# Copies and adds for the Strassen weight sums on new places, low parts of the first blocks on VectorE, and another order of the tail

## What is computed

```python
def first_block(x, p, ...):
    h = rmsnorm(x, g_pre)
    (qa, ka, va, gate_a, qi, ki, wi, qb, kb, vb, fb, gate_b) = split(h @ w_in)
    att_a = dsa_branch(qa, ka, va, qi, ki, wi)      # sparse attention, 8 heads
    att_b = fox_branch(qb, kb, vb, log_f)           # forgetting attention, 8 heads
    m_a, m_b = split(sigmoid(h @ w_merge))
    out = (m_a * (att_a * silu(gate_a)) @ w_branch_a + m_b * (att_b * silu(gate_b)) @ w_branch_b) @ w_out
    x = x + rmsnorm(out, g_post)
    return x + rmsnorm(sigmoid(x @ w_ple_gate) * (p @ w_ple), g_ple)

def second_block(x, ...):
    h = rmsnorm_2(x, mix_norm_g)
    qa, ka, va, q_lat, kv_lat, k_r, g_a, g_b = split(h @ w_in)
    o_a = swa_sink_attention(qa, ka, va, sinks)     # sliding window, 8 heads
    o_b = mla_attention(q_nope, q_rope, k_nope, k_rope, v)      # 8 heads
    y = sigmoid(g_a) * (o_a @ w_o_swa) + sigmoid(g_b) * (o_b @ w_o_mla)
    x = x + y @ w_out
    h = rmsnorm_2(x, ffn_norm_g)
    x = x + (silu(h @ w_gate) * (h @ w_up)) @ w_down            # d_ff 2816
    return rmsnorm_2(x, final_norm_g)
```

## Time and profile before

| What | Value |
|---|---|
| median of 3 runs | 1210.23 us (1209.99 to 1212.33) |
| the profiled execution | 1208.32 us, span 1206.5 us |
| PE busy | 1166.1 us, 97% of the span |
| DVE, ACT, POOL busy | 819.9 us (68%), 630.9 us (52%), 411.5 us (34%) |
[...]
| DMA: SP's queue, POOL's queue | 180.46 MB and 30.41 MB |

### The profile page before, as it was taken

How to read it: one execution, slowest core, us unless ns; L and a number is a source line. 1 busy time by engine, 2 the same in 40 slices (tenths; PEclk the granted TensorE clock), 3 DMA queues, 4 the chain that set the end, 5 groups by cost and what they waited for, 6 DMA issues and landing times.

```text
span 1206.5 us, 17475 instructions
## 1 busy us (share of the span) xinstructions
PE 1166.1 (97%) x6392; PEld 1000.5 (83%) x6392; DVE 819.9 (68%) x1663; ACT 630.9 (52%) x1105; POOL 411.5 (34%) x287
## 2 busy tenths in 40 slices
PE   9999999999999799999899999899989999999996
PEld 8878778888888687789778788688879999998885
DVE  5789874774628237699981775672599878786575
ACT  6553574476522345448683787333364454544454
POOL 1428462445544334312362676345435000000000
PEclk9999999999999899999999999999999999999998
DMA  8216773713998996555321402787546666667871
GB/s 276 79 63 244 210 244 141 227 53 140 287 274 230 298 280 192 163 207 147 106 39 37 140 1 69 213 208 176 138 156 199 206 204 202 205 218 256 312 261 70
DMA packets 91092, 216.30 MB, mean 179 GB/s; under 512 B 18424, under 2 KB 28152, under 8 KB 83968
## 3 DMA queue, kind: packets, MB, share of 16 engines
q1 hardware_dynamic: 83232, 180.46, 44.6%
q0 software_dynamic: 4608, 30.41, 12.4%
q10 hardware_dynamic: 3168, 4.33, 1.0%
HBM read 198.24 MB, written 71.45 MB: 224 GB/s over the span
## 4 chain that ended last, share of the span: by engine, by line
PE 71%; DVE 15%; DMA 4%; ACT 3%; issue 3%; POOL 2%; SPq 0%; ACTq 0%; DVEq 0%; POOLq 0%
PE bank L2302 38%; PE bank L2624 14%; PE bank L2638 8%; PE bank L2366 3%; PE bank L2398 2%; PE bank L2380 2%; PE bank L2444 2%; DVE sc L1789 2%; DMA w_raw<-in_w_out 1%; DVE m L1785 1%; DVE sqS L1935 1%; DMA w_raw<-in_w_o_mla 1%; POOL w_lo L907 1%; DVE t_lo L2023 1%; DMA rot<-in_rot 1%
## 5 line engine op out<-in xcount | busy, mean ns | idle before, releaser
L888 POOL TENSOR_TENSOR w_lo<-w_raw,w_hi 128x2048 fp32r<-128x2048 f32 (+4 forms) x49 | 218.1, 4451 | 366.3 <-ACT w_hi L992 311.8
L2302 PE MATMUL bank<-aH,w_hi 128*128 128x512 f32 x544 | 218.7, 402 | 2.6 <-DVE mqT L1986 1.0
L2302 PE MATMUL bank<-aH,w_lo 128*128 128x512 f32 x544 | 212.4, 391 | 0.0
L2302 PE MATMUL bank<-aL,w_hi 128*128 128x512 f32 x544 | 205.8, 391 | 0.0
L992 ACT ACTIVATE w_hi<-w_raw 128x2048 fp32r<-128x2048 f32 (+4 forms) x45 | 82.9, 1843 | 128.3 <-PE bank L2302 94.9
L2624 PE MATMUL bank<-t_hi,w_hi 128*128 128x256 f32 x504 | 143.5, 285 | 6.0 <-POOL w_lo L977 3.6
L2624 PE MATMUL bank<-t_hi,w_lo 128*128 128x256 f32 x504 | 143.1, 284 | 0.0
L2624 PE MATMUL bank<-t_lo,w_hi 128*128 128x256 f32 x504 | 143.1, 284 | 0.0
L2302 PEld LDWEIGHTS bank<-aH,w_hi 128*128 128x128 f32 x544 | 102.6, 189 | 22.2 <-issue 4.4
L2302 PEld LDWEIGHTS bank<-aL,w_hi 128*128 128x128 f32 x544 | 102.1, 188 | 22.3
L2302 PEld LDWEIGHTS bank<-aH,w_lo 128*128 128x128 f32 x544 | 102.5, 188 | 16.3
(11 more groups left out here) (414 smaller groups left out, 2687.2 us busy)
## 6 DMA issues: line engine op xcount, KB each, us to landing
w_raw<-in_w_in SPq DMA_DIRECT2D x21, 1024.0 KB, 5.0
w_raw<-up_sums SPq DMA_DIRECT2D x36, 512.0 KB, 4.3
w_raw<-in_gate_up SPq DMA_DIRECT2D x35, 512.0 KB, 4.2
up_sums<-in_gate_up SPq DMA_DIRECT2D x16, 1024.0 KB, 7.8
w_raw<-in_w_merge SPq DMA_DIRECT2D x8, 1024.0 KB, 5.0
up_sums<-in_gate_up POOLq DMA_DIRECT2D x8, 1024.0 KB, 11.6
up_sums<-up_sums POOLq DMA_DIRECT2D x8, 1024.0 KB, 10.8
w_raw<-in_w_out SPq DMA_DIRECT2D x8, 1024.0 KB, 7.3
```

Of the source, the lines that this page charges most:

```text
L888: pool.tensor_tensor(out=w_lo[:, c % 2, 0:n], in0=w_raw[:, c % 2, 0:n], in1=w_hi[:, c % 2, 0:n].bitcast(F32), op=ALU.subtract).then_inc(w_ ...
L2302: ins = pe.matmul(o, l, r, start=(kk == 0 and operand == ROUNDED and m == 0), stop=(kk == total - 1 and operand == REST), skip_group_check ...
```

## The change

It has four parts.

1. **Places of the copies and adds.** `COPY_AFTER` and `ADD_AFTER` get new values; a chunk may now stand several times in `COPY_AFTER`, and `ADD_AFTER` may name a row of an attention, behind whose scaling POOL issues the add. Copies now follow chunks 4 to 7, 9 to 11, 13 to 25, 46, 48, 50 and 54 (three each behind 7, 18, 46 and 54), so none between 26 and 45. Adds 3 to 7 stand in fox, 10 to 14 in dsa, 24 and 25 behind chunks 51 and 52, 26 to 30 in mla, 31 behind chunk 59; the others behind chunks 7 to 9, 15, 16, 19 to 26 and 33.
2. **Low parts at the Strassen start.** POOL ends with chunk 65. DVE makes the low part of chunk 66 ahead of the sums t_raw, and of blocks 0 to 6 like all others.
3. **Order at the Strassen start.** On ACT and DVE the splits of blocks 0 to 6, the operands and the gated products of pair 1 come in another order.
4. **Tail.** The finish of tokens 0 and 1, which stood ahead of step 19's splits, follows them; the finishes of all four blocks of tokens now run in order of n.

The diff, cut to its core:

```diff
-COPY_AFTER = (7, 8, 9, 10, 11, 12, 13, 14, 15, 16, 17, 18, 19, 20, 21, 22, 23, 24, 25, 26, 27, 28, 29, 30, 31, 33, 34, 35, 36, 38, 39, 40)
-ADD_AFTER = (15, 16, 19, 20, 21, 22, 23, 24, 25, 26, 27, 28, 29, 30, 31, 33, 34, 35, 36, 39, 40, 43, 55, 56, 57, 58, 59, 60, 61, 62, 63, 64)
+COPY_AFTER = (4, 5, 6, 7, 7, 7, 9, 10, 11, 13, 14, 15, 16, 17, 18, 18, 18, 19, 20, 21, 22, 23, 24, 25, 46, 46, 46, 48, 50, 54, 54, 54)
+ADD_AFTER = (7, 8, 9, ("fox", 6), ("fox", 12), ("fox", 18), ("fox", 24), ("fox", 30), 15, 16, ("dsa", 6), ("dsa", 12),
+             ("dsa", 18), ("dsa", 24), ("dsa", 30), 19, 20, 21, 22, 23, 24, 25, 26, 33,
+             51, 52, ("mla", 2), ("mla", 7), ("mla", 12), ("mla", 17), ("mla", 22), 59)
...
                 load(c)
-                if c in COPY_AFTER:
-                    copy_for_sum(COPY_AFTER.index(c))
+                for m in range(len(COPY_AFTER)):
+                    if COPY_AFTER[m] == c:
+                        copy_for_sum(m)
...
+            def adds_after(place_):
+
+                if place_ in ADD_AFTER:
+                    add_sum(ADD_AFTER.index(place_))
...
-                    if c in ADD_AFTER:
-                        add_sum(ADD_AFTER.index(c))
+                    adds_after(c)
...
                     pool.tensor_scalar(s, s, rsum[:, i:i + 1], 1.0, ALU.mult, ALU.mult).then_inc(scaled, 1)
+                    adds_after((name, i))
...
-            lo_through(len(CHUNKS) - 1)
-            for n in range(7):
-                pool.wait_ge(block_hi, n + 1)
-                pool.tensor_tensor(out=block_of(w_lo, n), in0=block_of(w_raw, n), in1=block_of(w_hi, n).bitcast(F32),
-                                   op=ALU.subtract).then_inc(block_lo, 1)
+            lo_through(len(CHUNKS) - 2)
...
+            block_high(0)
             first_high(0)
+            block_high(1)
             for i in range(4, 7):
                 t_high(i)
-            block_high(0)
-            block_high(1)
+            block_high(2)
+            block_high(3)
             silu(1)
-            block_high(2)
...
             for d in range(3, STEPS):
-                if d == STEPS - 1:
-                    for n in range(2):
-                        fin_square(n, 0)
-                        fin_square(n, 1)
-                        fin_root(n)
-                        fin_first_half(n)
                 down_high(d)
...
-                if 7 <= n < BLOCKS:
+                if n < BLOCKS:
                     dve.wait_ge(block_hi, n + 1)
-                    dve.wait_ge(block_lo, n)
                     minus(block_of(w_lo, n), block_of(w_raw, n), block_of(w_hi, n).bitcast(F32)).then_inc(block_lo, 1)
...
+            dve.wait_ge(w_lo_ready, n_chunks - 1)
+            dve.wait_ge(w_hi_ready, n_chunks)
+            minus(w_lo[:, (n_chunks - 1) % 2, :], w_raw[:, (n_chunks - 1) % 2, :],
+                  w_hi[:, (n_chunks - 1) % 2, :].bitcast(F32)).then_inc(w_lo_ready, 1)
...
             for d in range(3, STEPS):
-                if d == STEPS - 1:
-                    dve.wait_ge(small_landed, 48)
-                    for n in range(2):
-                        fin_add(n, 0)
-                        fin_add(n, 1)
-                        fin_gain(n)
-                        fin_scale(n)
                 down_low(d)
...
-            fin_add(2, 0)
-            fin_add(2, 1)
+            fin_add(0)
+            fin_add(1)
+            fin_gain(0)
+            fin_scale(0)
+            fin_gain(1)
+            fin_scale(1)
+            fin_add(2)
             fin_gain(2)
-            fin_add(3, 0)
             fin_scale(2)
-            fin_add(3, 1)
+            fin_add(3)
             fin_gain(3)
             fin_scale(3)
```

More of the change, by code:

```diff
@@ L867, in _, with add_sum @@
             pool.wait_ge(w_lo_ready, 2)
+            def add_sum(m):
+                table, c0, n = SUM_STEPS[m // 4]
+                to, _, kind, other = table[m % 4]
+                pool.wait_ge(sum_copied[m // 4], 64)
+                if kind == SUM:
+                    pool.wait_ge(sum_added[m % 4 - 2 if m % 4 == 2 else 2], 16 * (m // 4 + 1))
+                pool.dma_start(given_or_sum((SUM, to), table, c0, n), given_or_sum((kind, other), table, c0, n),
+                               accum_op=ALU.add).then_inc(sum_added[m % 4], 16)
+            def adds_after(place_):
+                if place_ in ADD_AFTER:
+                    add_sum(ADD_AFTER.index(place_))
             def lo_through(c_end):
@@ L1476, in _ @@
                     late(f - 1)
-                block_high(n + 5)
+                    block_high(n + 5)
                 block_high(n + 6)
@@ L2123, in _ @@
             operands(0, products(0))
+            block_low(0)
             t_low(2)
             first_low(0)
+            block_low(1)
             t_low(3)
+            t_low(4)
             gates_out(1, fg, 0)
-            for i in range(4, 7):
-                t_low(i)
             gates_out(1, fu, 2)
@@ L2136, in _ @@
                 block_low(n + 3)
-                made = products(f - 1)
+                if f > START:
+                    made = products(f - 1)
+                else:
+                    t_low(5)
+                    t_low(6)
                 block_low(n + 4)
@@ L2142, in _ @@
                     empties(minus(uu[:, g, :], fm1[:, g, :], bank_of(f"q6.{f}", g)[:, 0:HT]), f"q6.{f}", g)
-                operands(f - 1, made)
-                block_low(n + 5)
-                first_low(f - 1)
-                block_low(n + 6)
+                if f > START:
+                    operands(f - 1, made)
+                    block_low(n + 5)
+                    first_low(f - 1)
+                    block_low(n + 6)
+                else:
+                    block_low(n + 5)
+                    operands(f - 1, products(f - 1))
+                    block_low(n + 6)
+                    first_low(f - 1)
                 for g in range(2):
@@ L2229, in _, with fin_add, fin_gain, fin_scale @@
                             at = xr[:, first_token + i, S * column:S * column + S]
-                            ins = add(at, at, m1[:, i, :])
-                            if not extra:
-                                link(ins)
-            fin_add(2, 0)
-            fin_add(2, 1)
+                            add(at, at, m1[:, i, :])
+            dve.wait_ge(small_landed, 48)
+            low_at, high_at = slice(0, S), slice(S, D)
+            def fin_add(n):
+                b, i = (n + 2) % NB, n % 2
+                for half, at in enumerate((low_at, high_at)):
+                    product = "p7" if n < 2 else ("p2", "p3")[half]
+                    wait_filled(dve, product, i)
+                    (minus if n < 2 and half else plus)(xr[:, b, at], xr[:, b, at], bank_of(product, i)[:]).then_inc(fin_sum, 1)
+            def fin_gain(n):
+                b = (n + 2) % NB
+                dve.wait_ge(fin_sq, 2 * n + 1)
+                dve.tensor_scalar(qs[:, 0, 4 + b:5 + b], qs[:, 0, b:b + 1], 1.0 / D, EPS,
+                                  ALU.mult, ALU.add).then_inc(fin_bias, 1)
+                mult(xr[:, b, low_at], xr[:, b, low_at], gfin[:, low_at]).then_inc(fin_ready, 1)
+            def fin_scale(n):
+                b = (n + 2) % NB
+                dve.wait_ge(fin_rms, n + 1)
+                dve.reciprocal(qs[:, 1, 4 + b:5 + b], rT[:, b:b + 1]).then_inc(fin_inv, 1)
+                dve.wait_ge(fin_inv, n + 1)
+                dve.wait_ge(fin_sum, 2 * n + 2)
+                dve.scalar_tensor_tensor(out=xr[:, b, high_at], in0=xr[:, b, high_at], scalar=qs[:, 1, 4 + b:5 + b],
+                                         in1=gfin[:, high_at], op0=ALU.mult, op1=ALU.mult).then_inc(half_scaled[1], 1)
+            fin_add(0)
[5 more added lines that the diff above has]
+            fin_add(2)
             fin_gain(2)
-            fin_add(3, 0)
             fin_scale(2)
-            fin_add(3, 1)
+            fin_add(3)
             fin_gain(3)
```

70 lines of the change are left out of this document (17 added, 53 removed).

## The result

The changed kernel takes 1214.15 us (median of 11 runs, 1210.72 to 1219.41) against 1210.58 us for the kernel before (11 runs, 1205.20 to 1212.33) on the same chips: a ratio of 1.0038, with a 95% interval of 1.0021 to 1.0055. It is slower by 0.4%, where 1202 us and "faster" were forecast.

The account below looks back on a forecast made before the run. TensorE, busy 1166.1 us or 97% of the span, was taken as the bound. Gains of 24.1 and losses of 15.5 us turned 1208.3 into 1199.7 us profiled, about 1202 beside the median; range 1189 to 1214.

Parts of the forecast that it names:

- the price of the adds in fox: Forgetting attention: adds six rows apart, POOL mostly ahead of PE, which hides an issue; loss 1 us (0 to 3).
- waits on fox's head loads of over 2 us: Sign against the forecast: in the forgetting attention PE waits over 2 us for loads of a head.
- wo1: First output projection, second half: load freed of copies and adds lands earlier, 6.4 us wait and its spell go; gain 7.9 us.
- zb0: MLA output projection: load without the add beside it takes 10.4 or 11.5 us instead of 14.9; gain 5.0 us.
- MLA: MLA rows: each add held until the one before lands, delaying head 1's split and row 3; loss 11.5 us (8 to 14).
- The half-clock spell behind that stall: MLA, behind the late row 3: a stretch at half the granted clock, priced at 0 to 2 us.
- The rival that the chain never catches up: MLA's adds 24 to 30 run serially and stay late; at 12 us an add, 1220 us; slower case, chance 0.15.
- The sparse attention: Rows of dsa: an add held by the previous one delays row 7, 1 us more at row 12; loss 3 us (2 to 4.5).
- the Strassen start: First Strassen pair: low parts on DVE instead of POOL remove 6.0 us of PE waits; gain 6.4 us, 3 if DVE is late.
- the tail: End of kernel: last step's split goes ahead of the finish of tokens 0 and 1; gain 4.8 us (4 to 6.7).
- The rival that POOL does not wait for landings: All three attentions: fifteen moved adds cost only some 4 us of issues, 1190 us beside the median; chance 0.17.
- The eight pairs: Kernel before: an add's landing and the next add's issue 0.3 us apart, taken as evidence that POOL waits for landings.

## Why the prediction was wrong

**The step that failed** is the price of the adds in fox: "POOL is mostly 1 to 3 us ahead of PE, which hides an issue: 1 us (0 to 3, if the head loads are slowed)". It measured 13.2 us by the trace and 12.2 by leaving the adds out. The step asked what an add does to POOL, the engine on which it stands, and there it was right: PE's waits on POOL's sp are 2.8 us, all of them in dsa and none in fox. What an add does to the other queue it put into the bracket, at 3 us or less, without a row for it. SP loads a head every four rows, and PE began the two heads that it waited for within 0.1 us of their last landing. The second wait, 3.9 us, is that of an add in a row: with it in flight the head's last loads take 8.0 us in place of 2.7, and PE waits for what its slack does not cover. The first wait, 4.2 us, has no term in the sum at all: it comes from the adds behind chunks 7 to 9, ahead of fox, which make the copy behind chunk 11 late and by it the head whose loads follow. Together 8.1 us of waits, and the half clock behind them cost another 5.0 (2.4 and 2.6). The prediction named "waits on fox's head loads of over 2 us" as what would prove it wrong. A row for their price was at hand: loads of 1 MB beside adds and other transfers took 14.9 and 18.07 us in place of 5.0, and the gains at wo1 and zb0 were computed from that very slowing. It was used where adds went away and not where they were put.

**MLA** was right in its mechanism and short in one term. Add 25 held to the landing of add 24, head 1's split late, add 26 held, row 3 late: each came, within a microsecond of the upper ends. Row 3's turn is at 711.79 in place of 691.02; less the 9.9 of the start of this stretch it is 10.9 us late, where 9.4 to 10.6 stood. The half-clock spell behind that stall, taken at 0 to 2 us, cost 2.6; the one at 700 to 704 lies ahead of the stall, within the 10.9. The rival that the chain never catches up did not happen: between the turns of row 3 and the last row the trace loses 3.6 us, with the spell's 2.6, so the later adds cost the 1 us that was forecast.

**The sparse attention** lost 4.6 us where 3 was forecast with 4.5 as the end: 2.2 us of wait at row 7, as walked through, and again a spell, of 1.7.

**The gains** were right at each place: 7.9 for wo1 and 5.0 for zb0 to the tenth, 6.7 for the Strassen start where 6.4 stood, and 6.5 for the tail where 4.8 stood. For wo1 and zb0 the way was right as well: their loads took 10.4 and 10.0 us in place of 18.07 and 14.9, and the arithmetic had said 10.4 for both, or 11.5 for the second. In the tail the finish of all four blocks of tokens took 1.6 us less behind the last split than the serial chain by hand.

**The rival that POOL does not wait for landings** fell in the trace of the changed kernel (0.3 us behind two landings above), and the run with the setting at 1024 shows that the landing as such is not what it waits for: there two adds were issued 1.9 and 6.3 us ahead of the landing of the one before. The eight pairs that the prediction counts are eleven in the trace of the kernel before.

**Why the loads wait.** The DMA queue's row on the page counts the packets of all 32 adds:

```profile
q0 software_dynamic: 4608, 30.41, 12.9%
```

4608 packets over 32 adds and 16 engines are nine for each add on each engine, as a mean. In the run with one add in fox every load behind it landed after it. That trace shows the packets as well: from 153 to 159 us POOL's queue moved 112 packets of this add (0.92 MB) and SP's queue, on which the loads had been issued since 152.7, 32 packets (0.07 MB); from 159 to 160.9, with the last 32 packets of the add, SP's queue moved 202 (0.36 MB). What makes the loads' packets wait no run shows: an add of another size was not tried, so the cause of the order of landings stays open; that an add in flight makes the loads late is shown by the runs (8.0 us in place of 2.7).

## What to carry to other kernels

A transfer has two prices: what its issue holds on its engine (0.8 to 0.9 us of POOL for an add in MLA), and what it makes late on the other queues while it is in flight (the loads of fK, 8.0 us in place of 2.7). When one is moved, list the transfers that will be in flight beside it and the slack of whoever waits for them, above all for small loads that are needed soon after their issue; a stage is a good place not because its engine has time, but because nothing in it waits for a transfer: a single add cost nothing in MLA and 4.5 us in fox. A transfer that is made late passes this on to what stands behind it on its own queue: the copy behind chunk 11 took 12.7 us in place of 7.1, and the loads behind it 6.3 in place of 2.6 to 3.5. And the five waits of 2.2 to 5.0 us priced here each came with a half-clock spell, which cost another 1.7 to 2.6 us by the windows (a wait of 2.3 us for DVE, ahead of the sliding-window attention, had none in this trace: 1.00 from 575 to 600 us): only the part of a spell in which TensorE is busy counts, for losses as for gains.

## What the runs showed of the hardware

- A 1 MB accumulating transfer on POOL's queue made the 128 KB loads of fK on SP's queue, issued up to 5 us after it, take 8.0 to 8.2 us in place of 2.7 to 2.9; all landed within 3.5 us behind it.
- How many accumulating transfers were in flight at once in MLA depended on the setting dynamic_dma_scratch_size: with 512 the next was issued 0.3 us after the landing of the one ahead, with 1024 up to 6.3 us ahead of that landing. Two in flight at once, beside a load and three copies, took 11.4 and 13.1 us.
- One add among rows that wait for no transfer cost nothing: 1182.9 us with one in MLA, 1183.5 with it outside.
- The granted clock fell while TensorE was still waiting (0.50 from 141 to 142 us, the product at 142.53), so part of a half-clock spell cost nothing: 2.4 us of the first one in fox, which half of its 6.8 us would put at 3.4.
